# The last input block of a group is copied out of its bank before ScalarE's weight split, not after it

## What is computed

```python
h = rmsnorm(x, norm_g)
proj = h @ w_in                     # z (4096) | x, B, C (6144) | dt (64)
xbc, conv_new = causal_conv(xbc, conv_prev, conv_w, conv_b)   # width 4, then silu
y, s = ssd_chunk_scan(...)          # the recurrence, 64 heads in 8 groups
y = (y + xs * D_skip) * silu(z)
y = rmsnorm_of_each_group(y) * gate_norm
return x + y @ w_out
```

## Time and profile before

| | |
|---|---|
| time, median of 3 runs | 2325.52 us (2325.22 to 2327.51) |
| profiled execution: its own time | 2325.8 us |
| its span, first to last instruction | 2324.0 us |
| busy: PE / PEld | 2222.4 us (96%) / 1902.2 us (82%) |
| busy: DVE / ACT / POOL | 1348.7 (58%) / 1113.1 (48%) / 1078.9 us (46%) |
| mean granted clock of TensorE | 0.977 |
| longest group on POOL: `w_lo`, line 703 | x218, mean 2500 ns |
| ACT's split, line 915 | x216, mean 1050 ns |
| DVE's taps, line 1089 | x144, mean 970 ns |

### The profile page before, as it was taken

How to read it: one execution, slowest core, us unless ns; L and a number is a source line. 1 busy time by engine, 2 the same in 40 slices (tenths; PEclk the granted TensorE clock), 3 DMA queues, 4 the chain that set the end, 5 groups by cost and what they waited for, 6 DMA issues and landing times. The chain is left out here.

```text
span 2324.0 us, 39399 instructions
## 1 busy us (share of the span) xinstructions
PE 2222.4 (96%) x13958; PEld 1902.2 (82%) x13958; DVE 1348.7 (58%) x2193; ACT 1113.1 (48%) x2840; POOL 1078.9 (46%) x712
## 2 busy tenths in 40 slices
PE   6999999999999999899998996999999999999799
PEld 5999989898989898699996874777777777777599
DVE  5766676767676767653125667565565655655510
ACT  4455544545454545553344454554554544545322
POOL 5665656565656565266770004533333323333165
PEclk8999999999999999899999996999999999999899
DMA  4564646464656566234442312202112122021544
GB/s 163 199 218 158 230 161 227 166 223 170 221 173 221 172 219 211 104 126 158 146 163 105 127 53 82 72 22 71 55 40 62 31 63 72 21 72 34 223 161 135
DMA packets 80349, 309.83 MB, mean 133 GB/s; under 512 B 14578, under 2 KB 21874, under 8 KB 54690
## 3 DMA queue, kind: packets, MB, share of 16 engines
q1 hardware_dynamic: 80162, 307.38, 39.5%
HBM read 279.56 MB, written 27.79 MB: 132 GB/s over the span
## 5 line engine op out<-in xcount | busy, mean ns | idle before, releaser
L703 POOL TENSOR_TENSOR w_lo<-raw,w_hi 128x1024 fp32r<-128x1024 f32 x218 | 540.3, 2500 | 369.4 <-ACT w_hi L915 369.3
L122 PE MATMUL bank<-h_hi,w_hi 128*128 128x304 f32 x1776 | 552.2, 311 | 15.7 <-DVE h_lo L334 6.2
L124 PE MATMUL bank<-h_hi,w_lo 128*128 128x304 f32 x1776 | 538.8, 303 | 0.0
L123 PE MATMUL bank<-h_lo,w_hi 128*128 128x304 f32 x1776 | 536.5, 302 | 0.0
L122 PE MATMUL bank<-b_hi,a_hi 128*128 128x512 f32 x896 | 363.0, 405 | 21.1 <-POOL a_lo L2447 8.2
L915 ACT ACTIVATE w_hi<-raw 128x1024 fp32r<-128x1024 f32 x216 | 216.6, 1050 | 343.5 <-PE bank L124 343.5
L122 PEld LDWEIGHTS bank<-h_hi,w_hi 128*128 128x128 f32 x1776 | 335.9, 189 | 30.9 <-DVE h_lo L334 7.7
L123 PE MATMUL bank<-b_lo,a_hi 128*128 128x512 f32 x896 | 356.2, 398 | 0.0
L124 PE MATMUL bank<-b_hi,a_lo 128*128 128x512 f32 x896 | 355.4, 397 | 0.0
L123 PEld LDWEIGHTS bank<-h_lo,w_hi 128*128 128x128 f32 x1776 | 337.0, 190 | 2.3 <-issue 1.7
L124 PEld LDWEIGHTS bank<-h_hi,w_lo 128*128 128x128 f32 x1776 | 336.5, 189 | 0.0
(11 more groups left out here) (384 smaller groups left out, 3941.7 us busy)
## 6 DMA issues: line engine op xcount, KB each, us to landing
raw<-in_a_units SPq DMA_DIRECT2D x112, 1024.0 KB, 5.1
raw<-in_b_in_units SPq DMA_DIRECT2D x20, 1024.0 KB, 4.9
past<-in_cache SPq DMA_DIRECT2D x64, 288.0 KB, 3.3
pt<-in_cache_t SPq DMA_DIRECT2D x64, 256.0 KB, 2.6
raw<-in_o_units SPq DMA_DIRECT2D x16, 1024.0 KB, 5.1
s_in<-in_state_in SPq DMA_DIRECT2D x31, 512.0 KB, 7.0
out_state_out<-s_in SPq DMA_DIRECT2D x31, 512.0 KB, 6.8
s_t<-in_state_t SPq DMA_DIRECT2D x15, 1024.0 KB, 6.4
```

The source lines that it names most:

```text
L122: nc.tensor.matmul(out, a[0], b[0], start=start, stop=False)
L123: nc.tensor.matmul(out, a[0], b[1], start=False, stop=False)
L124: return nc.tensor.matmul(out, a[1], b[0], start=False, stop=stop)
L703: nc.gpsimd.tensor_tensor(w_lo[u % 2][:, c], raw[u % 2][:, c], w_hi[u % 2][:, c].bitcast(F32), ALU.subtract).then_inc(lo_done, 1)
```

## The change

```diff
                 for n in range(4):
+                    if g and n == 0:
+                        evac(*of_g[first_in - 1])
                     split(u + first_in + n + 1)
-                    if n == 0 or g == 0:
+                    if g == 0:
                         evac(*of_g[first_in + n - 1])
                     start(g, n)
```

## The result

The changed kernel takes 2342.60 us, the median of 4 runs (2339.33 to 2344.12); the kernel before took 2325.37 us beside it (4 runs, 2323.10 to 2327.51). The ratio is 1.0072, with a 95% interval of 1.0055 to 1.0090: the change makes the kernel 0.7% slower, about 17 us. The forecast was 2342, in a range of 2339 to 2350.

The account below looks back on a forecast made before the run. PE, busy 96% of the span, was taken to bound the kernel. Six boundaries at 2.47 us plus 1.8 us for the first gave 16.6 us on the 2325.5 us median: 2342 us, range 2339 to 2350.

Parts of the forecast that it names:

- The copy: Sixth boundary: ACT's copy of c 5 ends at 784.79, o 1 starts on its due time, gaining 1.24 us.
- The shift of POOL: Sixth boundary: POOL's two halves come 0.47 us later, the first starting at 785.82.
- Taps 0 and 1: Sixth boundary: both DVE taps end only behind POOL's halves; o 4 starts at 791.57, leaving 0.19 us of gain.
- Tap 3 is caught: Sixth boundary: DVE's tap 3, issued 0.41 us behind POOL's next start, is held and ends at 794.77.
- The small copy is caught: Behind tap 3, L1094 is held to 797.06 by POOL's second half; o 6 waits, boundary 2.47 us slower.
- The first boundary: POOL's next start and tap 3's issue tie; the loss is 2.9 or 0.7 us, with 1.8 us taken.
- The clock: Clock drops behind the o 6 waits cost nothing to 12 us; none taken, 7 us put into the range.
- That PE keeps the gain: Rival: all boundaries keep the time freed at o 1, 8.2 us less, 2317 us; chance 0.05.
- The rival by which tap 3 or its copy escapes: Rival of no change: 2324 us if both go free, 2328 if only the copy does; chance 0.10.

## Why the prediction was right

**The copy.** Right: it ended 0.79 us behind the start of o 0 (795.94), the forecast had 0.83, and o 1 started on its due time.

**The shift of POOL.** Right: 1.82 us behind o 0, forecast 1.86.

**Taps 0 and 1.** Right: 2.15 and 2.20 us. The addition of o 2 ended 7.53 us behind o 0 (forecast 7.56). The run with the copy between the halves leaves this shift out: o 4 starts 7.17 us behind o 0 there and not 7.58, tap 3 is issued in time, and 0.64 us are kept at each boundary.

**Tap 3 is caught.** Right, and this is the step that everything hangs on. The margin was smaller than thought: POOL started 8.13 us behind o 0 and not 8.05, tap 3 was issued at 8.42 and not 8.46, so 0.29 us lay between them, not 0.41. It is the end of o 3 that sets POOL's start, as the prediction had it, and not ACT, which stood idle for 0.55 us ahead of the split. With one more copy ACT fills that pause and nothing moves; with two, POOL starts 0.66 us later, and the tap is free. But the copy behind it is then caught still, and the kernel stays slower than before, 2330.1 us.

**The small copy is caught.** Right: 2.31 us (forecast 2.37). Three chains in group 0, far from the place of the change, carried this term, and the run with the small copies late shows that without it the answer would have been no change. With both caught, o 6 started 13.63 us behind o 0 (forecast 13.61), and the distance between the boundaries grew from 117.0 to 119.5 us, as forecast.

**The first boundary.** Here the sum took the middle of two ends, 1.8 us, and it was the low one, 0.64 us. The tap, issued at 206.53, won against POOL at 206.62 and ran free, and only the copy was caught:

```profile
206.53 0.55 DVE L1091 SCALAR_TENSOR_TENSOR cacc<-cbuf,conv_w,cacc 128x328 f32<-128x328 f32 x1
207.00 2.38 DVE L1096 COPY conv_new<-cbuf 128x24 f32<-128x24 f32 x1
```

**The clock.** The sum took no drop, and the profiled execution has one. Busy time by stretch (PE, PEld, DVE, ACT, POOL, then the granted clock, 0.50 being 1.2 GHz) behind the wait at o 6 of the second boundary, which was 2.44 us like the others:

```profile
330.00:333.30 3.30, 3.30 (x16) 3.27 (x15) 1.55 (x4) 0.00 (x0) 0.00 (x0) 0.50 0.70 283
```

It cost 1.6 us: 4.06 us at that boundary instead of 2.47. The two errors, 1.2 us too much at the first boundary and 1.6 us too little here, all but cancel by luck, so the measured time is nearer to the forecast than these two terms are. Twelve such waits stand in two profiles (six in the changed kernel, six in the run with one more copy for ACT), and the clock fell behind one of them. It fell too behind a wait of 2.79 us, at the first boundary of the run with two more copies for ACT. How often it falls in the runs that were not profiled isn't known, so the forecast's "none" was an assumption; it held at five of the six such waits of the profiled execution.

**The rivals.** That PE keeps the gain was rightly given little: in these runs it needed the taps moved, or POOL's subtractions replaced. The rival by which tap 3 or its copy escapes was made to happen, and the times are those worked out for it: 2324.4 us with both free (forecast 2324), and 2327.0 when tap 3 was caught and the copy did no harm (forecast 2328).

## What to carry to other kernels

Moving an instruction on an engine that has room still moves when its followers start. Here two small shifts met: POOL's first halves came 0.47 us later and held DVE's taps back, and PE, freed of its wait, let POOL's next half start 1.2 us nearer to o 0. Together they set POOL against tap 3 and the copy behind it, and PE lost 2.47 us a boundary where it had been due to gain 1.24 us. Where two engines hold each other up, list their instructions with start times side by side, and ask of each that is issued inside the other's what stands behind it. A short instruction can carry a long wait: put the ones that nobody waits for where the other engine is at rest, and move the long ones into pauses, before judging an edit that frees the bounding engine.

## What was not expected of the hardware

- Being small does not save a DVE instruction from being held. In the run with two more copies for ACT, at the first boundary, both small copies were held, one behind each of POOL's halves, and PE waited 2.79 us for them:

```profile
208.55 2.39 DVE L1099 COPY conv_new<-cbuf 128x24 f32<-128x24 f32 x1
...
210.86 2.37 DVE L1100 COPY conv_new<-cbuf 128x3 f32<-128x3 f32 x1
```

  The second copies 3 elements a partition, and was issued at the very time at which POOL's second half began, 210.86.
- Holding goes both ways, and the order of issue decides. Where tap 3 came 0.09 us ahead of POOL (first boundary of the changed kernel), POOL's half was shown as 2.73 us long instead of 2.40. The tap ran for 0.46 us into it; where it ran for 0.19 us into it (the run with the copy between the halves), POOL's half took 2.44:

```profile
206.62 2.73 POOL L703 TENSOR_TENSOR w_lo<-raw,w_hi 128x1024 fp32r<-128x1024 f32 x1 [1.85 <-ACT w_hi L915]
```
- The same wait of 2.4 us may or may not be followed by 3.4 us at the lower clock: one time in twelve here. Runs of the changed kernel lie between 2339.3 and 2344.1 us. The two longer ones have a mean granted clock of 0.977 and the two shorter ones 0.979, which fits the clock as the source of that spread; that it is the source was not tested.
